# Query tiles of the prompt's attention in reverse order in a one-core hybrid layer (mLSTM and differential attention) on Trainium2

## What is computed

```python
def diff_weights(scores, lam):
    p = jax.nn.softmax(scores, axis=-1)
    return p[:, :, 0] - lam * p[:, :, 1]

    def one_block(args):                       # blk: 0..3, 128 queries each
        qb, blk = args
        q_chunk = (blk * Q_BLOCK + jnp.arange(Q_BLOCK)) // CHUNK      # CHUNK = 64
        s = jnp.einsum('bqhcd,bkhcd->bhcqk', qb, k).astype(jnp.float32) * scale
        visible = key_chunk[None, :] <= q_chunk[:, None]
        s = jnp.where(visible, s, -jnp.inf)
        return jnp.einsum('bhqk,bkhd->bqhd', diff_weights(s, lam), vf)
```

## Time and profile before

| what | value |
|---|---|
| median of 3 runs | 1338.51 us (1335.16 to 1338.74) |
| the profiled execution's own time | 1338.28 us |
| its span in the trace | 1336.4 us |
| mean granted TensorE clock, share of 2.4 GHz | 0.982 |
| busy: TensorE matmul, its weight load, VectorE, ScalarE, GpSimd | 95%, 84%, 60%, 44%, 23% |
| stage of the prompt's attention, first scores to the sample's first scores | 736.4 to 783.4 us |

### The profile page before, as it was taken

One profiled execution on the slowest core, in us unless ns is written; L12 is line 12 of the kernel. 1 busy time (PEld: TensorE's weight loads), 2 busy tenths in 40 slices (PEclk: granted clock), 3 DMA queues, 4 the chain that ended last, 5 costly groups with the idle time before them and its releaser, 6 DMA issues.

```text
span 1336.4 us, 22947 instructions
## 1 busy us (share of the span) xinstructions
PE 1275.5 (95%) x8000; PEld 1124.8 (84%) x8000; DVE 804.4 (60%) x1457; ACT 582.0 (44%) x1148; POOL 313.0 (23%) x276
## 2 busy tenths in 40 slices
PE   4999999999999998999999788979999999999997
PEld 3899999999888877888877466869999999988886
DVE  3777776767544855343426764358766766754484
ACT  5634443434334756422213673355444443433463
POOL 0633434334100000010010413016444444310000
PEclk9999999999999999999998897989999999999999
DMA  9654545545357752321230433222323223134564
GB/s 316 200 158 150 164 141 158 153 145 156 110 173 252 270 188 56 123 87 63 95 111 11 133 111 116 64 81 78 94 79 94 78 79 93 39 121 165 195 219 141
DMA packets 167152, 175.84 MB, mean 132 GB/s; under 512 B 10377, under 2 KB 139921, under 8 KB 167098
## 3 DMA queue, kind: packets, MB, share of 16 engines
q1 hardware_dynamic: 165754, 171.31, 40.5%
q0 software_dynamic: 1344, 3.81, 0.9%
HBM read 165.79 MB, written 9.05 MB: 131 GB/s over the span
## 4 chain that ended last, share of the span: by engine, by line
PE 90%; ACT 4%; DVE 3%; DMA 2%; issue 1%; SPq 0%; ACTq 0%; DVEq 0%
PE ps L1261 86%; DMA w_raw_start<-in_w_ada 2%; DVE w_lo L1978 1%; PE ps L1321 0%; ACT x_norm L956 0%; PE ps L1856 0%; ACT squares L1154 0%; ACT probs L1164 0%; PE ps L1552 0%; PE ps L1290 0%; DMA k_cache<-in_cache_k 0%; PE ps L1607 0%; PE ps L1948 0%; DVE resid L2209 0%; PE ps L1822 0%
## 5 line engine op out<-in xcount | busy, mean ns | idle before, releaser
L1261 PE MATMUL ps<-h_sums_hi,w_sums_hi 128*128 128x320 f32 x1216 | 376.4, 314 | 3.4 <-ACT h_sums_hi L798 2.5
L1261 PE MATMUL ps<-h_sums_lo,w_sums_hi 128*128 128x320 f32 x1216 | 371.0, 309 | 0.0
L1261 PE MATMUL ps<-h_sums_hi,w_sums_lo 128*128 128x320 f32 x1216 | 371.0, 309 | 0.0
L1978 DVE TENSOR_TENSOR w_lo<-w_raw,w_hi 128x1024 fp32r<-128x1024 f32 (+2 forms) x106 | 145.5, 1373 | 199.4 <-ACT w_hi L920 124.3
L1261 PEld LDWEIGHTS ps<-h_sums_hi,w_sums_hi 128*128 128x128 f32 x1216 | 227.3, 188 | 14.2 <-issue 10.8
L1261 PEld LDWEIGHTS ps<-h_sums_lo,w_sums_hi 128*128 128x128 f32 x1216 | 227.6, 188 | 0.0
L1261 PEld LDWEIGHTS ps<-h_sums_hi,w_sums_lo 128*128 128x128 f32 x1216 | 227.4, 188 | 0.0
L860 ACT ACTIVATE silu_gate<-silu_gate 128x320 f32<-128x320 f32 x80 | 37.9, 473 | 285.5 <-DVE silu_gate L2105 285.5
L920 ACT ACTIVATE w_hi<-w_raw 128x1024 fp32r<-128x1024 f32 x88 | 93.2, 1059 | 142.4 <-PE ps L1261 128.9
L1978 DVE TENSOR_TENSOR w_sums_lo<-w_raw,w_sums_hi 128x512 fp32r<-128x512 f32 x132 | 112.4, 856 | 43.0 <-ACT w_sums_hi L856 42.2
L1261 PE MATMUL ps<-w_hi,h_t_hi 128*128 128x512 f32 (+2 forms) x360 | 135.3, 376 | 3.0 <-DVE h_t_lo L1978 2.0
(11 more groups left out here) (345 smaller groups left out, 1798.9 us busy)
## 6 DMA issues: line engine op xcount, KB each, us to landing
w_raw<-in_w_ffn_out SPq DMA_DIRECT2D x88, 512.0 KB, 3.7
w_raw<-in_w_ffn_in SPq DMA_DIRECT2D x86, 512.0 KB, 3.8
w_raw<-in_w_ada SPq DMA_DIRECT2D x22, 1024.0 KB, 5.0
w_raw<-in_w_in SPq DMA_DIRECT2D x10, 1024.0 KB, 5.1
w_raw_start<-in_w_ada SPq DMA_DIRECT2D x8, 1024.0 KB, 8.6
w_raw_late<-in_w_ada SPq DMA_DIRECT2D x6, 1024.0 KB, 6.9
w_raw<-in_w_out SPq DMA_DIRECT2D x4, 1024.0 KB, 5.0
k_cache<-in_cache_k SPq DMA_DIRECT2D x8, 512.0 KB, 4.9
```

The source lines that it names most:

```text
L1261: return pe.matmul(out, lhsT, rhs, start=start, stop=stop)
L1978: return dve.tensor_tensor(dst, raw, hi.bitcast(F32), ALU.subtract)
```

## The change

The 16 steps stay, and so does every instruction's place in its engine's program. A function maps a step to its query tile in reverse: steps 0 to 3 are now tile 3 (four blocks of keys), steps 4 to 7 tile 2, 8 to 11 tile 1, 12 to 15 tile 0 (one block). Banks and waits go by the step's number as before. What is woven in by step numbers stays at its steps.

```diff
+        def prompt_tile(n):
+            return NTP - 1 - n // HD
...
             def p_evac(n):
-                nk = P * (n // HD + 1)
+                nk = P * (prompt_tile(n) + 1)
...
-                        q = act.activation(HDF[:, n // HD, cols], PS[:, 6 + n // HD % 2, cols], ACT.Copy, scale=RSUM[:, n - HD + 1 + h, 0:1])
+                        q = act.activation(HDF[:, prompt_tile(n), cols], PS[:, 6 + n // HD % 2, cols], ACT.Copy, scale=RSUM[:, n - HD + 1 + h, 0:1])
...
             for n in range(NTP * HD):
-                nk = P * (n // HD + 1)
+                nk = P * (prompt_tile(n) + 1)
...
             def p_score(n):
-                t, h = n // HD, n % HD
+                t, h = prompt_tile(n), n % HD
...
-                for k in range(n // HD + 1):
+                for k in range(prompt_tile(n) + 1):
...
             def p_out(n):
-                t, h = n // HD, n % HD
+                t, h = prompt_tile(n), n % HD
                 pe.wait_ge(p_t, n + 1)
-                if t >= 2 and h == 0:
-                    pe.wait_ge(p_copied, t - 1)
+                if n >= 2 * HD and h == 0:
+                    pe.wait_ge(p_copied, n // HD - 1)
...
-                    q = mm(PS[:, 6 + t % 2, h * DV:(h + 1) * DV], PTT[:, n % 2, k * P:(k + 1) * P], DVT[:, k, h * DV:(h + 1) * DV], k == 0, k == t)
+                    q = mm(PS[:, 6 + n // HD % 2, h * DV:(h + 1) * DV], PTT[:, n % 2, k * P:(k + 1) * P], DVT[:, k, h * DV:(h + 1) * DV], k == 0, k == t)
...
             def p_maxima(n):
-                nk, m = P * (n // HD + 1), 8 * (n % 2)
+                nk, m = P * (prompt_tile(n) + 1), 8 * (n % 2)
...
             def p_combine(n):
-                nk, m = P * (n // HD + 1), 8 * (n % 2)
+                nk, m = P * (prompt_tile(n) + 1), 8 * (n % 2)
```

## The result

The changed kernel is slower, by about the amount that was forecast. Its median is 1343.3 us (14 runs, 1340.76 to 1355.19) against 1338.6 us of the kernel before (14 runs, 1335.16 to 1342.24) on the same chip: ratio 1.0039, 95% interval 1.0025 to 1.0054, or +4.7 us.

The account below looks back on a forecast made before the run. It took TensorE, 90% of the chain, to bound the kernel. Full-clock gain -1.5, low clock in the tail +3.0 and in the sample's attention +3.5 gave +5.0 on 1338.28: 1343.3 us, forecast's own range 1340 to 1347.5, overall 1335.5 to 1349.

Parts of the forecast that it names:

- Start, +2.15: Stage's first scores to first combine: four-block scores and two longer maxima put that combine 2.15 us later, at 744.6.
- Steps between: First combine to last at the full clock: 33.4 us in the new order against 33.1 of work before, order worth nothing.
- End, 3.9: Last combine's start to the sample's first scores: 3.9 us against 5.7, set by VectorE's weight split and keys' copy.
- the sample's first scores right behind the keys' copy: Sign in the trace at the stage's end: these scores follow VectorE's keys' copy directly, near 785, not 782.
- Clock, from about 771 to 791: Stage's end and sample's first steps: light TensorE work brings 1.2 GHz for 20 us; +3.0 up to the sample's first scores.
- Sample's attention, +3.5: Sample's attention starting at the low clock: two light steps +0.5 to 1.1 each, a full one +2.3, given as +3.5 us.
- The stage in sum, +1.5: Prompt's stage up to the sample's first scores: -1.5 us at the full clock and +3.0 for the low clock.
- Full clock total, -1.5: Stage at the full clock all the way: 744.6 + 33.4 + 3.9 = 781.9 against 783.43, 1.5 us faster.
- It moves as a whole: Sample's attention behind the stage at the full clock: same instructions, loads issued by its own steps, so it only shifts.
- The clock holds: Rival: full clock from 766 to 790, stage 1.5 us faster to 1 slower, 1336.8 to 1339, no change; chance 0.22.
- Low through the sample's attention: Rival: low clock stays through the sample's attention, 784 to 813.6, +13.5 us, 1352; chance 0.10.
- The fall at 813.6 does not come: Rival: the weak spot at 810 to 813.6 shifts and brings no low clock, -4.2 us, 1332.6 with clock holding earlier; chance 0.06.

Follow-up runs that it names:

- filled steps, split late: Changed kernel with one extra unread matmul ahead of the transposes of steps 8 to 15, and VectorE's weight split moved behind the sample's last steps: 1340.1 us, ratio 1.0019.
- squares early: Changed kernel with the norm's squares in steps 1 to 5 instead of 6 to 10: 1339.97 us; with extra unread matmuls behind the sample's attention too: 1336.21 us.
- the kernel filled in the steps and behind: Changed kernel with extra unread matmuls ahead of the transposes of its last eight steps and behind the sample's attention: 1338.2 us, ratio 0.9995.
- the clean pair: Changed kernel and kernel before, both with the same extra unread matmuls at the end of the sample's attention, same chip: 1340.24 against 1335.54 us.
- old order filled behind the sample: Kernel before with 12 extra unread matmuls in the waits between 811 and 822: 1335.88 and 1335.54 us in two runs, ratios 0.9984 and 0.9981.
- new order filled: Changed kernel with one extra unread matmul ahead of the transposes of steps 8 to 15 and three behind the last output: 1340.79 us, ratio 1.0009.

## Why the prediction was right, and where not

The forecast, 1343.3 us by a low clock for about 20 us over the end of the stage and the sample's first steps, came out in time, and the trace has that low stretch (20.5 us). The exact hit is luck: the parts were off by up to 2.3 us each, in both directions. It is also a hit of the medians; the pair of profiles that the sum was made for differs by 2.8 us.

- **Start, +2.15: right.** Where the clock did not fall ahead of the first combine (filled steps, split late), it came 8.31 us behind the first scores, against 6.09: +2.2. In the changed kernel it was +2.7, since a fall at 743.0 slowed the state update (2.83 us for four instructions, 2.33 before). The prediction held such a fall "as likely as not" and left it out of the sum; in these traces some short fall, 3.4 us long, began between 740 and 747 in every kernel of the new order. That was a term to put in, at 0.5 to 1.
- **Steps between: right.** Steps 8 to 11 took 2.44, 2.45, 3.37 and 2.35 for a forecast 2.45, 2.45, 3.35 and 2.35, and the last four at the full clock (squares early) 1.55, 1.41, 1.90 and 0.87 for 1.55, 1.4, 1.9 and 1.0.
- **End, 3.9: nearly the size, wrong cause.** It is 4.15 at the full clock, and set by ScalarE's key copy and head copies, which the late split shows. The prediction took "the stall that goes (heads' copies) is replaced by a shorter one (the split)"; the stall did not go, it began earlier. ScalarE's queue in the tail was not summed at all: that was the step left out. So the sign "the sample's first scores right behind the keys' copy" did not come: the copy began at 784.89 and took 0.69, the scores came at 786.56, released by the heads' copies. PE's own wait ahead of them, "nearly 2 us" in the prediction, is 1.6 by its two times (780.3 to 781.9) and was 1.28.
- **Clock, from about 771 to 791: right, 3 us late at both ends.** It was 773.8 to 794.2. The longest wait of PE in the 27 us ahead of it was 1.81 us. Ahead of the fall at 745 of the kernel before it was 1.77 us (of the first transposes, at 743.36), ahead of that at 813.6 it was 1.60. What makes the clock fall is shown by no run. The traces show what stood ahead of it: PE busy 2.11 of 3.44 us and 1.47 of 3.42 here, 1.77 of 3.41 and 1.79 of 3.40 before. That such a stretch brings the clock down was the author's estimate; with fills in it, or with the squares elsewhere, the 20.5 us did not come. The traces give the clock as a share of full speed (1.00, and 0.51 in the low windows) and no run shows it in GHz; the sums rest on the shares and on the times measured at each. In the steps and the tail it cost 2.9 for a forecast 3.0: from first combine to last, 35.24 less the 33.5 that the same steps take at the full clock, and 5.32 less 4.15. The 33.5 is from the kernel filled in the steps and behind, 34.31 less 0.75 for its fills.
- **Sample's attention, +3.5: right in size in the clean pair, +3.1, by two errors that cancel.** There 2.7 lies in two light steps of 1.35 each, where 0.5 to 1.1 each was forecast, and the full step, forecast at +2.3, was spared, as the clock came back ahead of it. Besides, the prediction's own terms add up to 3.3 to 4.5; why it took 3.5 it does not say. In the first pair of profiles only +1.3 showed: before, the last 4 us of this part ran at half the clock (0.51) themselves, and in the changed kernel they did not.
- **The stage in sum, +1.5: measured +2.3, and +2.45 in the clean pair.** The difference is the fall at the start, 0.5, and the tail, 0.5 (4.15 for 3.9, and 1.2 for 0.9 at the low clock), less some 0.3 in the steps, which the low clock slowed by 1.7 where 2.0 was forecast.
- **Full clock total, -1.5: not reached.** With the long low stretch taken away the stage took 46.2 and 46.7 us with the squares early, and 47.5 to 49.1 with fills in its steps, against 47.06 before: 0.8 us won at the best, and that with the 1.0 us of the moved squares in it. The short falls at its start or in its tail remained, and no kernel ran that had neither. The parts seen at the full clock in different traces, 8.31 + 33.5 + 4.15 = 46.0, would make it -1.1 (an estimate).
- **"It moves as a whole"** (the fall at 813 stays): not so in the profiled execution, probably so in most, as the gain by the fills and the clocks on record say.

The rivals. "The clock holds" did not come. The runs that made it hold, by fills or by moved work, lie at 1339.0 to 1340.8, up to 2 us above its 1336.8 to 1339. The fills' own time and the fall at the start are likely reasons. "Low through the sample's attention", 1352, did not happen in any trace: the longest low stretch, 20.5 us in two traces, ended at 794.2 and 793.6. One execution of 1355.19, with the lowest clock of the 14 (0.967), was not profiled; the kernel before also had single ones up to 1351.56, at 0.968. "The fall at 813.6 does not come" came true in the profiled execution, beside the forecast and not in its place.

## What to carry to other kernels

When light steps are moved behind one another, add up what TensorE does in each of them, with the other engines' stretching work on top, and look for stretches as light as those ahead of which the granted clock fell here (PE busy 1.47 of 3.42 us, 1.77 of 3.41, 1.79 of 3.40); then price the dense work that follows it, in the next stage too (here 3.1 us in the sample's attention). Tie side work (here the squares) to the steps in which TensorE is fullest, not to step numbers: when the order turns round, this work has to turn with it, and that alone was worth 4 us (1340.24 to 1336.21, in runs on two chips), some 1 us of it by shorter steps and the rest by the clock. And sum every queue of a tail, not only that of the engine one suspects.

## What was unexpected of the hardware

- **Twelve small matmuls in the waits of a light place saved some 3 us** (3.1 to 3.7 by the medians of three runs, 2.1 to 4.5 by their ratios), though two of the three intervals against the kernel before just reach 1 and the third gain compares runs on different occasions. With them, in the old order, PE was busy 14.57 of 15.0 us at the full clock from 813 on, where it had been 10.62 of 13.65 at half the clock (0.51).
- **The clock's falls near a light place shift or vanish from one execution or kernel to the next.** A wait of 1.83 us for a cached key's DMA was followed by 6.8 us at the low clock (0.54) in one kernel, a wait of 2.07 us at nearly the same place by none in another (1.00 from 797 to 812). Their PE rows, old order filled behind the sample, then new order filled:

```profile
798.45 1.09 PE L1856 MATMUL ps<-const,k_cache 128*128 128x128 f32 x8 [1.83 <-DMA k_cache<-in_cache_k]
```

```profile
799.37 1.09 PE L1866 MATMUL ps<-const,k_cache 128*128 128x128 f32 x8 [2.07 <-DMA k_cache<-in_cache_k]
```

- **The cached keys' loads are almost a bound.** PE waits for them between 796 and 812 in every trace that was looked at for it, 1.2 to 2.1 us in sum. Whether a stage that ends earlier finds them not yet landed, and how much of a gain ahead of them is lost there, was not tested by itself.
